# Moving a sample chain, convolution low halves, gathers and tables to later positions in a hand-ordered attention

## The reference

```python
def nsa_block(q, g, q_pos, kc, vc, kc_end, ks, vs, kw, vw, kw_pos):
    s_c = einsum('bqhgd,bnhd->bhgqn', qg, kc)               # compressed keys
    p_c = masked_softmax(s_c, kc_end[None, :] <= q_pos[:, None])
    o_c = einsum('bhgqn,bnhd->bqhgd', p_c, vc)
    score = ...                                             # p_c summed over heads and blocks
    _, idx = lax.top_k(where(forced, SEL_FORCE, ...), n_top)
    k_sel, v_sel = ks[bi, hi, idx], vs[bi, hi, idx]         # 16 blocks of 64 keys
    o_s = softmax attention over the selected blocks
    o_w = softmax attention over the last 512 keys
    return gq[..., 0:1] * o_c + gq[..., 1:2] * o_s + gq[..., 2:3] * o_w
```

## Time and profile before

| What | us |
|---|---|
| runs | 1282.66, 1284.52, 1292.17 |
| median | 1284.52 |
| the profiled execution | 1291.86 |
| its span | 1290.1 |
| TensorE busy | 1175.6 (91%) |
| VectorE busy | 714.8 (55%) |
| GpSimd busy | 416.1 (32%) |
| ScalarE busy | 380.2 (29%) |

### The profile page before, as it was taken

One profiled execution on the slowest core, in us unless ns is written; L12 is line 12 of the kernel. 1 busy time (PEld: TensorE's weight loads), 2 busy tenths in 40 slices (PEclk: granted clock), 3 DMA queues, 4 the chain that ended last, 5 costly groups with the idle time before them and its releaser, 6 DMA issues.

```text
span 1290.1 us, 17792 instructions
## 1 busy us (share of the span) xinstructions
PE 1175.6 (91%) x7124; PEld 946.5 (73%) x7124; DVE 714.8 (55%) x1363; ACT 380.2 (29%) x804; POOL 416.1 (32%) x376
## 2 busy tenths in 40 slices
PE   5889999999998789988999999899889999978995
PEld 4878999999888444544555545588589999966883
DVE  2567889998845686454454554643525640083432
ACT  3111111222234446345354554511101121162000
POOL 3443510000025653433234333354312211134444
PEclk9999999999999689798899999999989999988998
DMA  7552511423201300210400302532121111041321
GB/s 219 187 172 99 180 34 34 166 87 112 45 9 43 131 1 1 86 78 1 163 1 26 139 2 99 146 103 84 47 75 56 37 49 49 0 169 33 114 86 37
DMA packets 78008, 103.13 MB, mean 80 GB/s; under 512 B 21248, under 2 KB 64392, under 8 KB 76831
## 3 DMA queue, kind: packets, MB, share of 16 engines
q1 hardware_dynamic: 69839, 67.52, 16.9%
q0 software_dynamic: 6016, 33.56, 6.8%
q10 hardware_dynamic: 2080, 1.05, 0.3%
HBM read 90.42 MB, written 16.64 MB: 83 GB/s over the span
## 4 chain that ended last, share of the span: by engine, by line
PE 81%; DVE 9%; ACT 4%; POOL 2%; issue 2%; DMA 1%; POOLq 0%; ACTq 0%; DVEq 0%
PE PS L681 24%; PE PS L1576 15%; PE PS L1721 14%; PE PS L1137 6%; PE PS L1024 5%; PE PS L1151 4%; PE PS L673 2%; PE PS L1113 2%; PE PS L1072 2%; DVE ACC L548 2%; PE PS L1067 1%; ACT PRW L1177 1%; PE PS L1745 1%; DVE PS L1228 1%; DVE XL L1846 1%
## 5 line engine op out<-in xcount | busy, mean ns | idle before, releaser
L681 PE MATMUL PS<-XH,WH 128*128 128x352 f32 (+1 forms) x648 | 149.2, 334 | 3.1 <-DVE XL L523 3.1
L595 DVE SCALAR_TENSOR_TENSOR Y<-U,SM,Y 128x1024 f32<-128x1024 f32 x120 | 147.2, 1290 | 0.3
L681 PE MATMUL PS<-XL,WH 128*128 128x352 f32 (+1 forms) x648 | 143.5, 326 | 0.0
L681 PE MATMUL PS<-XH,WL 128*128 128x352 f32 (+1 forms) x648 | 143.2, 325 | 0.0
L681 PEld LDWEIGHTS PS<-XH,WH 128*128 128x128 f32 (+1 forms) x648 | 108.8, 188 | 6.5 <-DVE XL L523 3.8
L681 PEld LDWEIGHTS PS<-XL,WH 128*128 128x128 f32 (+1 forms) x648 | 110.4, 187 | 1.4
L681 PEld LDWEIGHTS PS<-XH,WL 128*128 128x128 f32 (+1 forms) x648 | 110.3, 187 | 1.4
L290 POOL TENSOR_TENSOR WL<-WRAW,WH 128x1024 fp32r<-128x1024 f32 x12 | 28.6, 2383 | 243.3 <-ACT WH L362 243.3
L1024 PE MATMUL PS<-PT,TM 128*64 128x256 f32 x528 | 91.8, 428 | 12.2 <-ACT PT L1168 6.0
L1576 PE MATMUL PS<-WOH,XH 128*128 128x512 f32 (+1 forms) x288 | 92.5, 403 | 10.8 <-DVE XL L1860 6.4
L548 DVE SCALAR_TENSOR_TENSOR ACC<-PS,SM,ACC 128x508 f32<-128x508 f32 x124 | 84.0, 740 | 31.0 <-PE PS L673 31.0
(11 more groups left out here) (297 smaller groups left out, 2124.3 us busy)
## 6 DMA issues: line engine op xcount, KB each, us to landing
WRAW<-in_w_in_even SPq DMA_DIRECT2D x16, 512.0 KB, 3.8
WRAW<-in_w_in_odd SPq DMA_DIRECT2D x16, 512.0 KB, 3.9
XIN<-in_x_prompt SPq DMA_DIRECT2D x8, 512.0 KB, 11.9
WRAW<-in_w_in_even SPq DMA_DIRECT2D x16, 256.0 KB, 3.7
TM<-in_state_win_kv SPq DMA_DIRECT2D x8, 512.0 KB, 4.8
XR<-in_x_prompt SPq DMA_DIRECT2D x8, 512.0 KB, 3.6
layer_out<-R SPq DMA_DIRECT2D x8, 512.0 KB, 2.6
XR<-layer_out SPq DMA_DIRECT2D x8, 512.0 KB, 3.4
```

What stands on the lines that cost most here:

```text
L595: v.scalar_tensor_tensor(dst, src, CWT[:, i, t:t + 1], dst, ALU.mult, ALU.add).then_inc(s_cv, 1)
L681: ins = pe.matmul(PS[0:mcols, 3 * slot + c, 0:CH], w[:, slot, kk, 0:mcols], x[:, kk, c * CH:(c + 1) * CH], start=(kk == 0 and n == 0), sto ...
```

## The change

The sample queries are made from the list, at position 20, and not ahead of the attention. `FIRST_H` goes from 4 to 20, and the pieces that are inserted by position (`H` 0 to 3, the first gather, `prep`, and now `prep2` in one row with them) stand from `FIRST_H` + 12 in steps of seven. The first piece of the ranking is due 10000 of the planner's nanoseconds behind its predecessor and not 2000.

In the new list, of 670 entries, `queries` stands at 20, `H` at 32, 39, 46 and 53, `csc` at 34, `gs` at 58, `gather` 0 at 60, `pct` at 66, `prep` at 67, `prep2` at 74, the ranking at 102, 108, 114, 121, 129 and 135, the first key transposition at 143, the last sample values at 642 and the last turn at 667. The first turn, T0, is at 15 and was at 21, in both as TensorE's next piece behind pair 5.

```diff
--- before.py
+++ after.py
@@ -893,7 +893,7 @@
         PV_PARTS = 4
         SAMPLE = [(("csc",), 6000, 1600), (("cmax",), 0, 0), (("cexp",), 0, 0), (("cnorm",), 0, 0),
                    (("gs",), 4000, 600), (("take", ("gs",)), 0, 0), (("pct",), 1500, 300), (("take", ("pct",)), 0, 0)]
-        SAMPLE += [(("rank", a, n), 2000, 0) for a in range(2) for n in range(3)]
+        SAMPLE += [(("rank", a, n), 2000 if a or n else 10000, 0) for a in range(2) for n in range(3)]
         for gi in range(4):
             for i in range(5):
                 for b in (2 * gi, 2 * gi + 1):
@@ -926,7 +926,7 @@
         at_ns, pair, since, later, to_exp, to_rcp, scaled = 0, 0, 0, [], [], [], -1
         nxt_sample, sample_at = 0, SAMPLE[0][1]
         LAG = 5000
-        FIRST_H = 4
+        FIRST_H = 20
         while pair < NP or todo or nxt_sample < len(SAMPLE):
             if pair == NP and not todo:
                 at_ns = max(at_ns, sample_at)
@@ -974,9 +974,9 @@
         ORDER += later
 
 
-        for n, x in enumerate([("H", i) for i in range(4)] + [("gather", 0), ("prep",)]):
-            ORDER.insert(FIRST_H + 2 * n, x)
-        ORDER.insert(FIRST_H + 40, ("prep2",))
+        ORDER.insert(FIRST_H, ("queries",))
+        for n, x in enumerate([("H", i) for i in range(4)] + [("gather", 0), ("prep",), ("prep2",)]):
+            ORDER.insert(FIRST_H + 12 + 7 * n, x)
 
         NB = 4
         row_bank, row_waits, holder, nxt = [], [], {}, 0
@@ -1332,6 +1332,8 @@
                     i = ev[1]
                     v.wait_ge(s_ah, i + 1)
                     v.tensor_tensor(XL[:, i, :], Y[:, i, :], XHf[:, i, :], ALU.subtract).then_inc(s_al, 1)
+                elif ev[0] == "queries":
+                    dve_queries(v, link)
                 elif ev[0] == "prep2":
                     dve_prep(v, link)
                 else:
@@ -1889,7 +1891,6 @@
             act_out(act, 1)
 
         def dve_late(v, link):
-            dve_queries(v, link)
             dve_attention(v, link)
             dve_join(v)
             dve_out(v, link, 0)
```

## The result

The kernel after takes 1301.3 us (median of 4 runs, 1298.80 to 1302.89), beside 1286.29 us for the kernel before on the same chip. The ratio on record is 1.0106, with a 95% interval of 1.0074 to 1.0139: it is slower. (The two medians alone give 1.0117; the four runs of the kernel before lie from 1282.66 to 1292.17, and I go by the ratio, 13.6 us.) I had predicted 1277.7 us in 1269 to 1287. A second series, run last, gave 1299.39 us and 1.0101 [1.0072, 1.0131]. The profiled execution took 1298.80 us (span 1296.9) against 1291.86. Its slices, to be held against the earlier trace rows, hold one digit less for TensorE in the 17th, 21st, 25th and 30th and one more in the 13th, and less for its clock in the 13th, 18th, 22nd and 30th and one more in the 19th.

A forecast was written before the change was run, and what follows sets the result against it. TensorE was taken to bound the kernel, except where it waits or runs at 1.2 GHz, both at the attention's start. -7.6 + 2.0 + 0.3 - 1.5 = -6.8 us, from 1284.52 to 1277.7; own range 1273 to 1282, with rivals 1269 to 1287.

The forecast's parts named there:

- Parts 1 and 2: Head of the attention: work leaves the first turns' chain; T0 7.4 us earlier, second turn 7.8; gain booked 7.6.
- the optimistic end of that term: Moving the queries lets the first exponential start at 414.06, the table load's end, not 414.94: 0.88 us.
- Part 3: Moved work behind the head: subtractions at positions 32 to 53 lose 2.0 us, gathers and tables on GpSimd 0.3.
- Part 4: Ranking's six pieces at positions 102 to 135: gain of 1.5 us, ends a gain of 5 and a loss of 5.
- Part 5: Attention's tail: last sample values come later, output weights' loads still hidden, cost 0 with 9 us of cover.
- B: Slower: ranking before wider minima lets TensorE run dry at positions 102 to 135, clock falls; +5.1 us, 1289.6; chance 0.10.
- the sign that I gave for B: A new stretch at 0.5 of TensorE's clock during the ranking would show B right.
- A: Moved work hands the gain back: subtractions cost 5.0 us, tables 1.5 before pair 15; -1.4 us, 1283.1; chance 0.18.
- C: Denser first-tile work lifts TensorE's clock, one half-clock stretch goes, 5 to 7 us more; -12.8, 1271.7; chance 0.16.
- D: Start unmoved: ScalarE's table load and bank waits set T0, which moves less than 2 us; 1284; chance 0.06.
- Three of the signs that I named: 900-wide comparisons in the 460s; first sample key turn about 10 us after 477.3 less head's gain; attention's end about 809.

The follow-up runs named there:

- e7: e4 with prep moved ahead of the compressed scores and prep2 later still: 1283.45 us, ratio 0.9970 against the kernel before.
- e4: Kernel after with the first ranking piece due at 2000 again and prep2 farther behind, at 97: ratio 0.9978 against the kernel before.
- e3: Kernel after with prep2 moved farther behind prep (97 instead of 74): ratio 1.0037 against the kernel before.
- e2: Kernel after with the first ranking piece due at 2000 again, all else as changed: ratio 0.9999 against the kernel before.
- e1: Kernel before with only the first ranking piece's due time changed from 2000 to 10000: ratio 1.0085.
- e5: Kernel before with all sample pieces at the places of due time 10000, the prompt's own sequence kept: ratio 1.0070.
- e8: As e5, but the pieces up to the ranking's end kept at their early places: ratio 1.0077 against the kernel before.
- h kernels: Kernel before with the first sample group's pieces moved as a block by -4, 4, 10 and 16 prompt pieces: ratios 1.0015, 1.0001, 1.0056, 1.0074.
- g1: Kernel before with the first ranking piece due after 4000 in place of 2000: ratio 1.0097.

## Why the prediction was wrong, point by point

**Parts 1 and 2, the head: right.** T0 was to come 7.4 us earlier, it came 7.6 (13.6 less 6.0 behind the first scores). The head's gain was put at 7.6 and is 8.9 at T1. The chain named what I said would leave it. The first exponential came forward to the table load's end, which was the optimistic end of that term. How much of it stays is less sure: e7's ratio shows 3.9 us, e4's 2.8 with an interval that reaches 0.

**Part 3, the moved work: the term that failed first.** The four subtractions were booked with +2.0. They lie at 424 to 434.6 us with 1.25 us each, where TensorE is at half clock up to 432 us and hardly idle; but all four stand in the chain that leads to prep2's wait, and no run moves them alone. In e4 and e7 they stand as late and the run is not slower than before, so they cost less than the head gives; their price stays open. (Beside the third, two of GpSimd's scalings took 1.95 us at 429.02, where two alone take 0.88.) prep2 was priced as "about 1.1 us" of VectorE's own time, with no term for a wait. I looked at where its operations would lie and not at what they wait for. With prep2 7 places behind GpSimd's tables instead of 30, the price was a wait of 2.69 us on VectorE, 4.89 us on TensorE behind it, and with what follows 0.7% of the run (after to e3), 9 us; with the early ranking 0.2% (e2 to e4), not clear of noise. The sum had 2.3 us for all moved work of both engines.

**Part 4, the ranking: the term with the largest error.** Forecast a gain of 1.5 us, ends -5 and +5; measured alone (e1) a loss of 0.85%, 11 us, outside both ends. The step that failed is "Its six pieces go from positions 79 to 116 to 102 to 135". That is true, and I priced only these. In this planner a due time is not the place of one piece: everything behind moves, and the prompt's own order with it. The runs put 0.7 to 0.8% on the sample pieces behind the ranking, about 0.2% on the prompt's new sequence, and nothing measurable on the place that I had priced.

**Part 5, the tail: right.** Cost 0, and the loads were covered.

**The rivals.** B had the sign, less than half of the size (+5.1 us against +13.6), and another cause: a stretch of idle and half clock did come at 440 to 450 (from prep2), and one at 470 to 480, beside the second half of the ranking, so the sign that I gave for B came true; but by e5 and e8 the ranking's own place is not what costs. A's subtractions are not priced by any run (its sum has a term of -0.3 without a source; with the forecast's -1.5 for the ranking it would be 1281.9). That the kernel could be slower by more than 1% had a chance of 0.03 in the text. C fell: TensorE was busy 10.94 of 11.0 us from 415 us and was granted 0.50 all the same, as in the earlier trace rows. D fell, since the start moved as told. Three of the signs that I named: the 900-wide comparisons start at 456.9 us, 47.9 behind the first scores, at the early edge of what I told; the first sample key turn at 482.9, 73.9 behind them, where I wanted 67.5; and the last values end 415.1 behind them, where I wanted 397. So about 6 us of the 18 that the end is late are lost ahead of the first key turn, and 12 behind it.

**Why the range was too narrow.** It was made of ends for parts that each have a place. There was no term for the list as a whole, although the text itself had the last values 17 positions later, and used that for the tail alone. The h kernels and g1 show what such a term has to be: from nothing to 1% of the run, with a size that cannot be told from the shift. None of the shifts measured was a gain.

## What to carry to other kernels

In a list made by a planner with a running clock, changing one due time is a change to everything behind it: print both lists, compare the order of all pieces including those not edited, and price that as an unknown of its own size (here 0 to +1% of the run). A piece moved nearer to what it depends on, on another engine, gets a wait: count the places between producer and consumer, and what stands ahead of the producer on its engine. And where work is to be cleared out of a chain, keep the rest of the schedule fixed by moving pieces in the finished list, as e7 does.

## What the runs showed of the hardware

The small VectorE operation of prep2 with 4 columns took 1.20 us in the kernel after, when GpSimd's 900-column selection began in the same 10 ns:

```profile
442.73 1.20 DVE L1425 TENSOR_SCALAR SE<-SE 128x4 f32<-128x4 f32 x1
442.74 1.16 POOL L1443 TENSOR_SCALAR_AFFINE_SELECT LT<-LT 128x900 f32<-128x900 f32 x1
```

In the kernel before the same operation, with nothing of that kind beside it, took 0.23 us:

```profile
439.18 0.23 DVE L1423 TENSOR_SCALAR SE<-SE 128x4 f32<-128x4 f32 x1
```

The two ran as if one held the other for its whole length, here GpSimd holding VectorE, the other way round than in the earlier trace rows. It repeats: 1.20 us in both profiles of the kernel after and in e2, where the two meet, and 0.23 us in both profiles of the kernel before and in e1, e3, e4 and e7, where they don't. The Trainium skill (SBUF — State Buffer, "SBUF: two separate sides") describes such a lock between the two, held by whichever starts first; these rows agree with it and do not prove it.

Being busy did not bring TensorE the higher clock at the head: 415 to 426 us is 99% busy at 1.2 GHz in the kernel after, and 418 to 429 us in the kernel before, 40% busy, is at 1.2 GHz as well. And the stage ahead of the attention took up to 6 us more or less from one execution to the next with no edit in it, and went with the clock granted in the first 45 us (0.89 to 1.00), which is about half of the whole effect looked for.
